# Products of the state-space setup and the q, k scaling moved from GpSimd to VectorE, with new slots for the layer-0 side work

## The reference

```python
# layer 0
h = _rms(x, e_norm[j]); proj = h @ e_w_in[j]
u, z_s5, q, k, v, z_da = jnp.split(proj, e_splits, axis=-1)
y_s5 = _s5_mixer(u, ...) * jax.nn.silu(z_s5)
y_da = _diff_attention(q, k, v, ...) * jax.nn.silu(z_da)
x = x + jnp.concatenate([y_s5, y_da], axis=-1) @ e_w_out[j]
# inside _s5_mixer: a scan of h[t] = a * h[t-1] + (B u)[t], complex, a = exp((lr + i li) dt)
# inside _diff_attention: q = _rms(q, gain), k = _rms(k, gain), then softmax(q k), two parts subtracted
# layer 1
q, k, v, z, f_logit = jnp.split(_rms(x, o_norm[j]) @ o_w_in[j], o_splits, axis=-1)
x = x + (_forgetting_attention(q, k, v, ...) * jax.nn.silu(z)) @ o_w_out[j]
```

## Time and profile before

| | us |
|---|---|
| median of three runs | 1058.02 (1057.35 to 1058.29) |
| the profiled execution | 1058.58 |
| its span in the trace | 1056.9 |
| TensorE busy | 998.5 (94%) |
| VectorE busy | 636.7 (60%) |
| ScalarE busy | 565.8 (54%) |
| GpSimd busy | 179.6 (17%) |

### The profile page before, as it was taken

How to read it: one execution, slowest core, us unless ns; L and a number is a source line. 1 busy time by engine, 2 the same in 40 slices (tenths; PEclk the granted TensorE clock), 3 DMA queues, 4 the chain that set the end, 5 groups by cost and what they waited for, 6 DMA issues and landing times.

```text
span 1056.9 us, 14419 instructions
## 1 busy us (share of the span) xinstructions
PE 998.5 (94%) x5309; PEld 840.8 (80%) x5309; DVE 636.7 (60%) x923; ACT 565.8 (54%) x915; POOL 179.6 (17%) x143
## 2 busy tenths in 40 slices
PE   7969699699699699999999999999999999999998
PEld 7958487587587599987888877887888788878886
DVE  4699739749759657557555554555455545555453
ACT  5757555655556556645445555455544555455331
POOL 2142602603604500000000210031004001300000
PEclk9989799899899899999999999999999999999999
DMA  7945233333333433655589996565999955745562
GB/s 261 202 128 180 88 111 101 119 100 120 113 101 106 119 101 121 231 168 199 188 169 175 171 162 172 160 190 149 155 164 161 187 167 150 208 130 169 199 217 82
DMA packets 112737, 163.62 MB, mean 155 GB/s; under 512 B 19125, under 2 KB 52010, under 8 KB 112426
## 3 DMA queue, kind: packets, MB, share of 16 engines
q1 hardware_dynamic: 98256, 159.41, 57.2%
q10 hardware_dynamic: 14426, 3.48, 1.8%
HBM read 160.76 MB, written 2.10 MB: 154 GB/s over the span
## 4 chain that ended last, share of the span: by engine, by line
PE 59%; issue 19%; DVE 15%; ACT 4%; POOL 2%; DMA 0%; ACTq 0%; DVEq 0%; POOLq 0%
PE bank L433 14%; PE bank L435 13%; PE bank L434 13%; DVE wl L914 4%; PE bank L452 3%; PE bank L454 2%; PE bank L453 2%; DVE scr L1537 2%; ACT wh L906 2%; DVE scr L1548 2%; PE bank L676 1%; PE bank L661 1%; POOL con L2004 1%; PE bank L490 1%; PE bank L645 1%
## 5 line engine op out<-in xcount | busy, mean ns | idle before, releaser
L914 DVE TENSOR_TENSOR wl<-raw,wh 128x1024 fp32r<-128x1024 f32 x296 | 369.5, 1251 | 328.3 <-ACT wh L906 327.2
L906 ACT ACTIVATE wh<-raw 128x1024 fp32r<-128x1024 f32 x296 | 311.5, 1056 | 194.2 <-PE bank L435 145.7
L433 PE MATMUL bank<-wh,xh 128*128 128x512 f32 x768 | 316.4, 412 | 12.9 <-DVE wl L914 12.9
L435 PE MATMUL bank<-wh,xl 128*128 128x512 f32 x768 | 303.9, 396 | 0.0
L434 PE MATMUL bank<-wl,xh 128*128 128x512 f32 x768 | 303.5, 395 | 0.0
L433 PEld LDWEIGHTS bank<-wh,xh 128*128 128x128 f32 x768 | 147.0, 191 | 44.4 <-DVE wl L914 13.9
L435 PEld LDWEIGHTS bank<-wh,xl 128*128 128x128 f32 x768 | 146.4, 191 | 33.0
L434 PEld LDWEIGHTS bank<-wl,xh 128*128 128x128 f32 x768 | 147.3, 192 | 27.3
L433 PE MATMUL bank<-wh,yh 128*128 128x512 f32 x256 | 100.9, 394 | 2.9 <-ACT scr L1299 1.7
L435 PE MATMUL bank<-wh,yl 128*128 128x512 f32 x256 | 99.8, 390 | 0.0
L434 PE MATMUL bank<-wl,yh 128*128 128x512 f32 x256 | 99.6, 389 | 0.0
(11 more groups left out here) (315 smaller groups left out, 1180.4 us busy)
## 6 DMA issues: line engine op xcount, KB each, us to landing
raw<-in_o_w_in SPq DMA_DIRECT2D x128, 512.0 KB
raw<-in_e_w_in SPq DMA_DIRECT2D x128, 256.0 KB
raw<-in_e_w_in SPq DMA_DIRECT2D x32, 512.0 KB
raw<-in_e_w_out SPq DMA_DIRECT2D x32, 512.0 KB
raw<-in_o_w_out SPq DMA_DIRECT2D x32, 512.0 KB
raw<-in_s_w_glu SPq DMA_DIRECT2D x8, 512.0 KB
res<-in_x SPq DMA_DIRECT2D x4, 512.0 KB, 6.9
res<-in_x SPq DMA_DIRECT2D x1, 2048.0 KB, 8.1
```

Source lines behind the costliest of these rows:

```text
L433: nc.tensor.matmul(o, l_hi, w_hi, start=first, stop=False)
L435: mm = nc.tensor.matmul(o, l_lo, w_hi, start=False, stop=last)
L906: nc.scalar.activation(wh[:, j % RING, :], raw[:, j % RING, :], ACT.Copy).then_inc(hi_done, 1)
L914: nc.vector.tensor_tensor(wl[:, j % RING, :], raw[:, j % RING, :], wh[:, j % RING, :].bitcast(F32), ALU.subtract).then_inc(lo_done, 1)
```

## The change

1. **Moved engine.** The three angle products, the powers of c, the multiplier `mg` and the scaling of q and k are now VectorE instructions. GpSimd keeps only the small powers of -0.5 (`out_norm`, `qk_norm`). A new semaphore `qk_rn` says that the power is there; VectorE scales and then signals `qk_ready`.
2. **Angles by batch.** They are done for 8 columns at a time, once in each of steps 0 to 3 (`TAB_SLOT` 9, 10), and so is ScalarE's `table` (slot 11); before, everything was done in step 0.
3. **Slots.** The powers of c are in slots 12 and 13, those of b in 14 and 15; transposes, `s5_near` and the rest of the state space move to slots 0 to 9 of the next step, GELU to 10 and 11, `s5_high` to 12, `s5_low` to 13. The attention begins in slots 14 and 15 of its own step (`QKT_SLOT` -2, -1), and its consumers on ScalarE and VectorE are a slot or two behind.
4. **v and z apart.** `vz_out` becomes `v_out_of` (slot 1) and `z_out` with the SiLU (slot 6).

```diff
-BA_SLOT, FAR_SLOT, TAB_SLOT = 8, (5, 9), 8
-T_SLOT = [12, 12, 13, 13]
-NEAR_SLOT = [14, 15]
-X_SLOT, YN_SLOT, Y_SLOT = [0, 1], 2, [3, 5]
-IN_SLOT, OUT_SLOT = [1, 3], [2, 4]
-GELU_SLOT, HIGH_SLOT = [9, 10], 11
-QKT_SLOT = [1, 2]
-SC_SLOT = [3, 4, 5, 6]
-EXP_SLOT = [5, 5, 6, 7]
-PT_SLOT = [7, 9]
-PV_SLOT = [8, 11]
-YT_SLOT = [12, 14]
+TAB_SLOT, FAR_SLOT, BA_SLOT = [9, 10], [12, 13], [14, 15]
+T_SLOT = [0, 0, 1, 1]
+NEAR_SLOT, HOLD_SLOT = [2, 3], 4
+X_SLOT, YN_SLOT, Y_SLOT = [4, 5], 6, [7, 9]
+IN_SLOT, OUT_SLOT = [5, 7], [6, 8]
+GELU_SLOT, HIGH_SLOT = [10, 11], 12
+QKT_SLOT = [-2, -1]
+SC_SLOT = [-1, 0, 1, 2]
+MIX_SLOT = [3, 5]
+PT_SLOT = [4, 6]
+PV_SLOT = [5, 8]
+YT_SLOT = [8, 11]
+SILU_SLOT = 6
...
             def table(k):
-                half = slice(16 * k, 16 * k + 16)
+                half = slice(TB * k, TB * k + TB)
...
+            def angles(k, part):
...
+                if part == 0:
+                    v.tensor_tensor(near_, every, wide(ph_all), ALU.mult)
+                    v.tensor_tensor(hi, every, wide(ph_hi), ALU.mult)
+                    link(v.tensor_tensor(lo, every, wide(ph_lo), ALU.mult))
+                else:
+                    link(v.tensor_scalar(near_, near_, MAGIC, None, ALU.add))
+                    link(v.scalar_tensor_tensor(out=w, in0=near_, scalar=-MAGIC, in1=hi, op0=ALU.add, op1=ALU.subtract))
+                    link(v.tensor_tensor(w, lo, w, ALU.subtract))
+                    v.tensor_scalar(w, w, 0.5, -0.5, ALU.min, ALU.max).then_inc(tab_ang, 1)
...
+            def s5_far(i, r):
...
+                times(ca_t[0], r, 0)
+                link(times(ca_t[1], 1 - r, 1))
+                for half in range(2):
+                    at = slice(64 * half, 64 * half + 64)
+                    o = ca[at, r, :, :].rearrange("p i (k h) -> p (i k) h", k=5)[:, :, 16 * half:16 * half + 16]
+                    ins = v.tensor_tensor(o, *(x[at].rearrange("p i k h -> p (i k) h") for x in ca_t),
+                                          ALU.subtract if r else ALU.add)
...
+            def s5_hold(i):
...
+                link(v.tensor_tensor(mg[:, :, :], x, y, ALU.mult))
...
+            def qk_norm(i, t):
+                dve.wait_ge(qk_rn, i * NT + (t + 1))
...
+                v.tensor_tensor(x, x, rn.to_broadcast([P, n, 64]), ALU.mult).then_inc(qk_ready, 1)
```

More of the change, by code:

```diff
@@ L1023, in s5 @@
                 i, at = s // (2 * UNITS), s % (2 * UNITS)
-                if i + 1 < DA_PAIRS:
+                if i + 1 < DA_PAIRS and at == TAB_SLOT[1] + 1:
+                    table(i + 1)
+                if i >= 0:
                     for k in range(4):
                         if T_SLOT[k] + 1 == at:
-                            s5_turned(i + 1, k)
+                            s5_turned(i, k)
                     for h in range(2):
                         if NEAR_SLOT[h] + 1 == at:
[L1030 to L1033, removed]
                             s5_near(i, h)
@@ L1081, in setup @@
                 chunk_tokens(1, s)
[L1082 to L1085, removed]
+                if s in (6, 8):
+                    c_out((s - 6) // 2)
             def gate():
@@ L1515, in lam_end, with wide @@
                 link(v.tensor_scalar(nlam, nlam, LAMBDA_INIT, None, ALU.add))
[L1517 to L1527, removed]
+            def angles(k, part):
+                batch = slice(TB * k, TB * k + TB)
+                every = steps.rearrange("p (i c) -> p i c", i=1).to_broadcast([P, TB, NCH])
+                def wide(x):
+                    return x[:, batch].rearrange("p (i c) -> p i c", c=1).to_broadcast([P, TB, NCH])
+                (hi, lo), near_, w = tab_t, cos_t[:, batch, :], sin_t[:, batch, :]
+                if part == 0:
+                    if k == 0:
+                        dve.wait_ge(steps_done, 1)
+                    v.tensor_tensor(near_, every, wide(ph_all), ALU.mult)
[6 more added lines that the diff above has]
+                    v.tensor_scalar(w, w, 0.5, -0.5, ALU.min, ALU.max).then_inc(tab_ang, 1)
@@ L1604, in s5 @@
                 if i + 1 < DA_PAIRS:
[L1605 to L1608, removed]
+                    for part in range(2):
+                        if TAB_SLOT[part] == at:
+                            angles(i + 1, part)
+                        if FAR_SLOT[part] == at:
+                            s5_far(i + 1, part)
+                        if BA_SLOT[part] == at:
+                            s5_powers(i + 1, part)
                 if i >= 0:
+                    if at == 0:
+                        s5_skip(i)
+                    if at == HOLD_SLOT:
+                        s5_hold(i)
                     for h in range(2):
@@ L1622, in _ @@
             aside = {(0, 6): diagonal, (1, 0): log_steps, (1, 2): angles_ready, (1, 3): gains, (1, 4): turns,
-                     (1, 5): b_factors, (1, 6): powers, (2, 2): lam_end, (2, 3): b_blocks,
-                     (2, 5): lambda: angles(0), (2, 6): lambda: angles(1)}
+                     (1, 5): b_factors, (1, 6): powers, (2, 2): lam_end, (2, 3): b_blocks}
             def cols_out(c, at):
```

159 lines of the change are left out of this document (70 added, 89 removed).

## The result

The changed kernel takes 1050.4 us (1050.23 to 1050.49 in three executions), the kernel before 1058.1 in the same session: a ratio of 0.9923 with a 95% interval of 0.991 to 0.9936. A fourth execution of the changed kernel took 1917.55 us at a lower granted clock (0.939) and is left out. The profiled execution took 1050.3 us, with a span of 1048.5.

A forecast was written before the change was run, and what follows sets the result against it. It took VectorE's queue, lengthened by GpSimd's products, to bound steps 0 to 3. Losses of 58.2 us would become 10.3 + 40.5 = 50.8, a gain of 7.4 from 1058.58, so 1051 us; range 1045 to 1056.

The forecast's parts named there:

- the likeliest case: The changed kernel is measurably faster, below 1055.9 us; chance 0.68.
- The total of losses: TensorE's waits and slow clock over the whole kernel: 58.2 us before the change, 50.8 after.
- The setup: Near 57 to 64 us: without GpSimd's angle products VectorE's small products run fast and TensorE gains 9.9 us.
- The rate of the moved work: VectorE per step: 12.8 us added at uncontended rates, 8.5 removed, net +4.3, so 60 us busy.
- a plain addition: VectorE charged 12.8 us a step without credit: 69 us in a step, some +3 us a step.
- The new wait: Slot 14 of steps 1 to 3: TensorE waits 11.0 us for `yt_low`; loss with slow clock 13.5 a step.
- The slow clock: Matmuls run at half clock after a long wait in a step, costing 2.5 us each time.
- Step 0: Late `qk_ready`, `ba_done` and first maximum, plus slow clock: 10.3 us lost against 14.9 before.
- A looser chain: Steps 1 to 3: engines overlap better by way of ScalarE, waits of 5 us, not 11: 1033 us; chance 0.16.
- slow powers of c: Slots 12 and 13: powers of c stay slow on VectorE, 4.4 us more a step: 1068 us; chance 0.16.
- The setup's gain: Rival: the setup's 9.9 us do not come, the instructions being slow for something else: 1061 us; chance 0.05.
- the gain was not cancelled: Denies the rival that new and old losses cancel within 2 us, at 1.5 to 2.5 more per step: 1057; chance 0.11.

The follow-up runs named there:

- e6: Changed kernel with `yt_low` first in slot 13, table in 14, angles in 1, 2, powers of c in 11, 13, of b in 4, 10: 1001.8 us.
- e3: Changed kernel with GpSimd doing its old three angle products once more at their old place, results overwritten: 1062.5 us.
- e1: Changed kernel with ScalarE's table in slot 14, behind both halves of the GELU, instead of slot 11 between them: 1036.1 us.
- e2: Changed kernel with `yt_low` of the last head ahead of the powers of c in VectorE's slot 13: 1056.2 us.
- e4: Kernel before with only the powers of c moved to VectorE, in slots 12 and 13: 1043.6 us.
- e5: Kernel before with powers of c on VectorE in slots 10 and 12, and the three angle products there in slot 4 of step 0: 1016.7 us.
- e7: Changed kernel with the scaling of q and k back on GpSimd: 1050.2 us.
- e9: e6 with `yt_low` of the last head back behind the second half of the powers of c and `s5_low`: 1018.6 us.
- e8: Changed kernel with the edits of both e1 and e2: 1042.8 us.

## Why the prediction was right, step by step

Forecast 1051 for 1050.4; faster, as the likeliest case had it, with the gain as a difference of two large sums.

- **The total of losses.** Before was put at 58.2 us above a kernel without them, which is 1000.4. e6, with nearly none, takes 1001.8. After was put at 50.8; against e6's span it is 48.3. TensorE's own work in a step was put at 66 us and is 67.5 in e6; that is the same before and after.
- **The setup.** The cause was right (e3). The wait was 8.6 as read; with its slow matmuls it is worth 12.1, not 9.9. The term was 2.2 too small.
- **The rate of the moved work.** Half the powers of c was put at 3.3 us and takes 1.55 + 1.65 = 3.2. Products of 640 columns take 0.8, as forecast. VectorE's busy time from one waiting matmul to that of the next step was 55.9 and 56.3 us before (L516 to L516) and is 59.6 both times now (L475 to L475): +3.5, where +4.3 was forecast, and not the 12.8 of a plain addition. The 4.3 was 0.8 too much; the sum in us did not use it, only the judgement that VectorE has room.
- **The new wait.** Forecast 11.0 at L475 for L1743 with VectorE idle 6.5 ahead of its split; measured 11.68 and 6.63. The sum had 33.4 - 22.4. In the trace of step 2, counted from the start of unit 8 at 241.99, TensorE is done with unit 14 at 22.4, as forecast; ScalarE's split of slot 12 is done at 23.2 for 22.8, and VectorE needs 10.8 from there for 10.6. e1 took one link out and the wait fell by its length.
- **The slow clock.** 2.5 us was forecast for each of four falls, 10.0 in all; 8.3 came. Against e6, TensorE is busy 2.2, 1.2 and 1.6 us more in the stretches behind the three long waits, so 2.5 was too much there, and 4.1 more in step 0, where it was too little (0.9 less ahead of these). Since the two small lags behind it did not vanish altogether either (0.6 at L491 in step 2), the loss of a step is 80.7 - 67.5 = 13.2, for 13.5. The loss before is 77.3 - 67.5 = 9.8, for 10.9. The difference was put at 2.6 and is 3.4 a step.
- **Step 0.** 1.0, 5.0 and 1.8 were forecast for `qk_ready`, `ba_done` and `sc_max`; 1.2, 4.6 and 0.9 came. With the 4.1 of slow clock that is 10.8, for 10.3.
- **Together.** The steps were charged 3 x 0.8 = 2.4 us too little, and 3.5 too little was credited outside them (18.6 for 9.9 + 4.6 + 0.6 = 15.1). The errors nearly cancel, so a hit within 1 us is partly luck.
- **The rivals.** None happened. A looser chain (1033) would have shown waits of 5 us at L475; slow powers of c (1068) waits over 14. The setup's gain came, and the gain was not cancelled.

The Trainium skill (ScalarE: Activation LUTs, What ACT_TABLE_LOAD costs) counts a drain with each load. The GELU's first instruction starts 1.30 us after the start of a load that lasts 1.28, and e1's 4.35 us for two loads and three short instructions leave no room for one; the measurement decides. The prediction read the Trainium skill (Perfetto Trace Analysis, Optimizing Scalar/DVE Operations) as charging the moved work without a credit. That was not a fair reading: the Trainium skill states no price there, and it says in the same section that moving operations between VectorE and GpSimd might not help, because they share a port. The trace bears that caution out: taking the work back cost VectorE +3.5 and not +12.8 us a step.

What was wrong lay in the expectations of the experiments. e2 had the waits right (7.7, then about 2 and up to 2 more; measured 7.68, 1.71 and 1.72) and expected 1047 to 1050 us. The step that failed is the slow clock behind the later waits: it was put at nothing and made TensorE busy 7.5 us more. e4 put the wait at `s5_near` at 0 to 3 us a step; it is 5.5 in steps 1 to 3, because the powers of c stand in the slot right ahead of their user. e5 and e6 came out better than expected, by 7 and 4 us, and the 1.8 us of e7 did not come.

## What to carry to other kernels

An engine that works in order delays everything behind a long piece. So look at each place where the bounding engine waits, and ask what stands in the queue ahead of the instruction that it waits for; another engine can stand on that path too, as ScalarE's sine did here. Put long pieces that nobody needs yet behind short ones that somebody waits for. When everything in the queue is late, reordering only moves the wait (e2); when one piece is late alone, it removes it (e6 against e9). Before moving work between VectorE and GpSimd, price it at the rate of each engine alone and subtract what the one did to the other.

## What was not expected of the hardware

Several short waits of TensorE cost more than one long one. In after, four falls of the clock came with 8.3 us more busy time than e6 has. In e2, with nearly the same idle time (50.3 us of waits against 51.6), it was 15.8, and in e8 15.7. In e9, with three waits of only 4.3 us, it was 5.5. The granted clock in two stretches of 10 us, of after and of e2 (columns as in the earlier trace rows), in that order:

```profile
274.00:284.00 10.00, 7.96 (x33) 6.54 (x34) 9.67 (x16) 2.62 (x5) 0.00 (x0) 0.75 0.37 117
284.00:294.00 10.00, 9.37 (x49) 7.50 (x48) 7.07 (x14) 7.92 (x17) 0.00 (x0) 1.00 0.36 109
```

```profile
278.00:288.00 10.00, 8.24 (x36) 6.14 (x35) 9.67 (x16) 3.29 (x5) 0.00 (x0) 0.89 0.34 107
288.00:298.00 10.00, 8.32 (x33) 6.67 (x34) 5.55 (x12) 6.41 (x16) 0.00 (x0) 0.83 0.35 105
```

After is back at full clock within 3 us of the long wait; e2 falls to half again at its two waits of 1.7 us. Over the three steps, TensorE is busy for 12.5 us at the lower level (0.50) behind the waits of 11.7 us in after, and for 12.6 us behind those of 7.7 in e2, so the shorter wait saved nothing of this. Behind its later waits e2 has another 12.1 us. But not every short wait does it: in e5 the clock stays at full through the waits of 1.4 us at L516 in steps 1 to 3. What makes the difference is not shown here.

And a VectorE product of 32 columns lasts until the GpSimd instruction beside it is done. In e3 three of them end at 61.33, 64.92 and 68.49; GpSimd's first ends at 61.27 and its last at 68.44. In these rows it is not a lower rate but a standstill. The Trainium skill (SBUF — State Buffer, Who interferes with whom) says that a VectorE instruction with two inputs in SBUF contends with a GpSimd instruction that reads SBUF, over a port pair that is locked and not shared out. These rows agree, 3.6 us for 0.19. Others do not: in after a VectorE instruction with two inputs of 128x512 (L1535) takes 0.69 us wholly inside a GpSimd power of 128x8 that lasts 2.55 (from 250.31), and 0.69 is what products of that size take without GpSimd beside them (L1532, just ahead of it).
